# The first layer of the compression by three products per pair of units, and five K steps per turn

## What is computed

```python
def compress(rows, pos_emb, w1, w2):          # rows: B, L, groups (2), 64
    n_units = L // CMP_STRIDE                 # units of 16 tokens
    n_cmp = n_units - CMP_UNITS + 1           # a block is two adjacent units
    units = rows[:, :n_units * CMP_STRIDE].reshape(B, n_units, CMP_STRIDE, G, D)
    blocks = jnp.concatenate([units[:, j:j + n_cmp] for j in range(CMP_UNITS)], axis=2)
    hid = jax.nn.silu(jnp.einsum('bnlgd,lde->bnge', blocks + pos_emb[:, None, :], w1))
    return jnp.einsum('bnge,ef->bngf', hid, w2)
```

## Time and profile before

| | |
|---|---|
| time, median of 3 runs | 790.75 us (786.97 to 792.52) |
| span of the profiled execution | 792.1 us |
| TensorE busy | 735.8 us, 93% of the span |
| VectorE, ScalarE, GpSimd busy | 55%, 26%, 10% |
| DMA | 220.72 MB, mean 279 GB/s |

### The profile page before, as it was taken

How to read it: one execution, slowest core, us unless ns; L and a number is a source line. 1 busy time by engine, 2 the same in 40 slices (tenths; PEclk the granted TensorE clock), 3 DMA queues, 4 the chain that set the end, 5 groups by cost and what they waited for, 6 DMA issues and landing times.

```text
span 792.1 us, 14734 instructions
## 1 busy us (share of the span) xinstructions
PE 735.8 (93%) x4779; PEld 356.7 (45%) x4779; DVE 438.4 (55%) x945; ACT 206.8 (26%) x524; POOL 82.9 (10%) x155
## 2 busy tenths in 40 slices
PE   7999999999999999998999996898897887999997
PEld 3465645453545456443544562334443452433542
DVE  3351250805704357997563838957768656645273
ACT  0411011102010213122233323534455334333200
POOL 0000000000000000020002016500746200000000
PEclk9999999999999999998999997999999976999999
DMA  8997987999898989979788129988899939984621
GB/s 327 306 319 214 339 279 253 298 353 351 296 371 282 378 314 365 373 262 390 254 282 279 37 92 305 334 304 275 250 317 318 296 131 387 364 280 142 262 112 55
DMA packets 134552, 220.72 MB, mean 279 GB/s; under 512 B 17642, under 2 KB 58771, under 8 KB 133259
## 3 DMA queue, kind: packets, MB, share of 16 engines
q1 hardware_dynamic: 113754, 194.75, 71.7%
q0 software_dynamic: 6080, 13.25, 5.0%
q10 hardware_dynamic: 14640, 11.77, 4.8%
HBM read 213.84 MB, written 10.04 MB: 283 GB/s over the span
## 4 chain that ended last, share of the span: by engine, by line
PE 57%; DVE 17%; SPq 10%; DMA 8%; issue 4%; ACT 2%; POOL 0%; ACTq 0%; DVEq 0%
PE banks L652 13%; PE banks L630 13%; SPq L428 8%; PE banks L905 4%; PE banks L1036 4%; PE banks L666 4%; DMA proj<-in_cmp_cache 3%; PE banks L1157 3%; DVE att L1863 3%; DMA ring<-in_dv_cache 3%; PE banks L934 2%; PE banks L976 2%; PE banks L952 2%; DVE banks L1862 1%; PE banks L969 1%
## 5 line engine op out<-in xcount | busy, mean ns | idle before, releaser
L652 PE MATMUL banks<-ring,xt 128*128 128x512 f32 (+1 forms) x448 | 188.4, 574 | 0.0
L652 PEld LDWEIGHTS banks<-ring,xt 128*128 128x128 f32 x448 | 83.8, 192 | 93.8 <-issue 91.1
L630 PE MATMUL banks<-proj,wide 128*64 128x256 f32 x896 | 99.9, 384 | 2.2 <-DMA proj<-in_cmp_cache 2.1
L1382 ACT ACTIVATE wide<-banks,att 128x384 f32<-128x384 f32 (+3 forms) x128 | 66.4, 524 | 133.4 <-DVE att L1863 132.2
L630 PEld LDWEIGHTS banks<-proj,wide 128*64 128x64 f32 x896 | 66.3, 139 | 38.2 <-DMA proj<-in_cmp_cache 5.8
L905 PE MATMUL banks<-ring,small 128*32 128x512 f32 x512 | 71.6, 640 | 4.9 <-DMA ring<-in_dv_cache 3.3
L1589 DVE TENSOR_SCALAR small<-small 128x510 f32<-128x510 f32 x8 | 3.4, 427 | 122.8 <-ACT small L1227 106.3
L1212 ACT ACTIVATE proj<-banks,x_rs 128x512 f32<-128x512 f32 (+1 forms) x32 | 21.2, 664 | 177.0 <-PE banks L652 142.1
L666 PE MATMUL banks<-ring,small 128*32 128x512 f32 x512 | 61.4, 598 | 2.1 <-DMA ring<-in_dk_cache 2.0
L934 PE MATMUL banks<-proj 64*128 64x384 f32 (+7 forms) x256 | 54.7, 505 | 6.9 <-ACT wide L1382 6.9
L446 POOL DMA_DIRECT2D ring<-in_sel_cache x104 | 55.4, 533 | 32.9 <-issue 28.9
(11 more groups left out here) (360 smaller groups left out, 829.9 us busy)
## 6 DMA issues: line engine op xcount, KB each, us to landing
ring<-in_dk_cache SPq DMA_DIRECT2D x256, 256.0 KB, 5.7
ring<-in_dv_cache SPq DMA_DIRECT2D x256, 256.0 KB, 5.5
proj<-in_cmp_cache SPq DMA_DIRECT2D x144, 128.0 KB, 3.9
ring<-in_w_in SPq DMA_DIRECT2D x6, 2048.0 KB, 12.1
proj<-in_cmp_cache ACTq DMA_DIRECT2D x80, 128.0 KB, 5.4
ring<-in_x_nat SPq DMA_DIRECT2D x2, 2048.0 KB
ring<-in_cmp_cache SPq DMA_DIRECT2D x32, 128.0 KB, 4.2
ring<-in_w_out SPq DMA_DIRECT2D x2, 2048.0 KB, 11.9
```

The costliest lines, as they stand in the source:

```text
L630: last = mm(to, w1[:, kv, half, lp, :], rows[:, kv, g, lp, :, :, :], start=lp + half == 0, stop=lp == LP - 1 and half == 1, tile_position= ...
L652: last = mm(banks[:, 3 + n % 2, 0:width(c)], xt[:, k, P * t:P * t + P], w_ring[:, c % 2, k, 0:width(c)], start=k == 0, stop=k == KC - 1)
L1382: last = A(e_slot(j, c)[:, 0:n], banks[:, 2 * (j % 2) + c, 0:n], ACT.Exp, bias=row_max[:, j % 4, c:c + 1], accum_out=row_sum[:, j % 4, c:c ...
```

## The change

The units are paired: even unit 2m, odd unit 2m+1. Three products are taken: W1 on the even units (E), W0 on the odd ones (O), and W0 + W1 on their sum (S). Then block 2m+1 is O(m) + E(m+1), and block 2m is S(m) - O(m) - E(m). Each product has 16 matmuls of 256 columns (128 pairs x 2 groups); keys and values now go to the two column halves. The page layout in memory is changed on the host for this.

- first_layer(b) is the first two products. After two K steps first_sums(b) does the third, and only its last matmul signals pre_ready. It waits for units_summed.
- VectorE: sum_units(b) copies E out of PSUM and adds the odd units to the even ones in place (4096 columns); keep_pre(b) makes the sums and the difference in the hidden buffer; then the silu as before. W0 + W1 is made once, in the memory of the query blocks, which are cleared after sequence 7 instead of at the start.
- ScalarE's exponentials (and its half of the page loads behind them) wait for pre_kept, the last of these.
- The prompt's compression keeps both halves of w1, with 32 matmuls of 64 columns for 64 of 32.
- K_TURN is 5 instead of 6, K_LAST 5 instead of 4; the late tiles have 34 K steps over 13 tiles instead of 30 over 12. keep_scores(1), (3), (5), (6) and (7), silu_z(27) and sum_new(7) change places on VectorE, load_w(6) and load_w(7) on SyncE.

```diff
--- before.py
+++ after.py
@@ -128,9 +128,9 @@
-    w2b = z((2, 2, 64, 2, 64), w2.dtype)
-    w2b[:, 0, :, 0], w2b[:, 1, :, 1] = w2, w2
-    cmp_kv = x["cache_nsa_cmp_kv"][0].reshape(n_pool, 8, LP, 2, 2, NKV, HD)
+    w2b = z((2, 64, 2, 64), w2.dtype)
+    w2b[0, :, 0], w2b[1, :, 1] = w2[0], w2[1]
+    cmp_kv = x["cache_nsa_cmp_kv"][0].reshape(n_pool, 4, 2, LP, 2, 2, NKV, HD)
...
-        "w2": f(w2b.transpose(1, 2, 0, 3, 4).reshape(P, 2, P)),
-        "cmp_cache": f(cmp_kv.transpose(0, 3, 6, 4, 5, 2, 1).reshape(n_pool, P, 256)),
+        "w2": f(w2b.reshape(P, P)),
+        "cmp_cache": f(cmp_kv.transpose(0, 4, 7, 5, 3, 2, 1, 6).reshape(n_pool, P, 256)),
...
+        bias = sb("bias", [P, 2])
+        q_both = sb("q_both", [P, 1024])
...
+        w1_sum = q_both[:, :].rearrange("p (k l e) -> p k l e", k=2, l=LP)
+        q_nsa = q_both[:, 0:512].rearrange("p (b n) -> p b n", b=DEC)
+        q_sel = q_both[:, 512:1024].rearrange("p (q n) -> p q n", q=16)
...
-        K_STEPS, K_TURN, K_LAST = 64, 6, 4
-        K_LATE = (2, 2, 2, 2, 3, 3, 3, 2, 3, 3, 3, 2)
+        K_STEPS, K_TURN, K_LAST = 64, 5, 5
+        K_LATE = (2, 2, 2, 2, 3, 3, 3, 3, 3, 3, 3, 3, 2)
...
-                if n == 45:
+                if n == 41:
...
-                if n == 56:
+                if n == 53:
...
+            def cmp_rows_of(b):
+
+                return cmp_home[int(b == 1)].rearrange("p t (b k l q x) -> p k l q t b x", b=8, k=2, l=LP, q=2)
+
+            def first_product(b, bank, at, weights, parity):
+
+                for lp in range(LP):
+                    for kv in range(2):
+                        to = banks[64 * kv:64 * kv + 64, bank, at:at + 256].rearrange("p (t b x) -> p t b x", t=TILES, b=8)
+                        last = mm(to, weights[:, kv, lp, :], cmp_rows_of(b)[:, kv, lp, parity, :, :, :], start=lp == 0, stop=lp == LP - 1,
+                                  tile_position=(0, 64 * kv), skip_group_check=True)
+                return last
+
...
                 if b > 0:
-                    pe.wait_ge(s("hid_ready"), b)
-                rows = cmp_home[int(b == 1)].rearrange("p t (g k h l n) -> p k h l t g n", g=8, k=2, h=2, l=LP)
-                for kv in range(2):
-                    for lp in range(LP):
-                        for half in range(2):
-                            for g in range(2):
-
-                                to = banks[64 * g:64 * g + 64, kv, 1 - half:1 - half + UNITS].rearrange("p (t b n) -> p t b n", t=TILES, b=8)
-                                last = mm(to, w1[:, kv, half, lp, :], rows[:, kv, g, lp, :, :, :], start=lp + half == 0,
-                                          stop=lp == LP - 1 and half == 1, tile_position=(0, 64 * g), skip_group_check=True)
-                last.then_inc(s("pre_ready"), 1)
+                    pe.wait_ge(s("pre_kept"), b)
+                first_product(b, 0, 0, w1[:, :, 1, :, :], 0).then_inc(s("even_done"), 1)
+                first_product(b, 1, 0, w1[:, :, 0, :, :], 1).then_inc(s("odd_done"), 1)
+
+            def first_sums(b):
+
+                pe.wait_ge(s("units_summed"), b + 1)
+                first_product(b, 0, 256, w1_sum, 0).then_inc(s("pre_ready"), 1)
...
+            first_sums(0)
...
+            first_sums(1)
...
+                first_sums(b)
...
+                    for lp in range(LP):
+                        for half in range(2):
+                            for kv in range(2):
+                                to = banks[64 * kv:64 * kv + 64, 5, 256:384].rearrange("p (g n) -> p g n", g=2)[:, :, 1 - half:1 - half + P_UNITS]
+                                rows = p_rows[:, :, :, 16 * kv:16 * kv + 16].rearrange("p t u (g l) -> p l g t u", g=2)[:, lp, :, :, :]
+                                last = mm(to.rearrange("p g (t u) -> p g t u", t=TILES),
+                                          w1_again[:, 2 * kv + half, HD * lp:HD * lp + HD], rows,
+                                          start=lp + half == 0, stop=lp == LP - 1 and half == 1, tile_position=(0, 64 * kv),
+                                          skip_group_check=True)
...
 
-                act.wait_ge(s("pre_ready"), b + 1)
-                if b > 0:
-                    act.wait_ge(s("hid_ready"), b)
-                for kv in range(2):
-                    last = A(sig[:, kv, 0:NCMP], banks[:, kv, 1:1 + NCMP], ACT.Exp, bias=bias[:, 1, kv:kv + 1], scale=-1.0)
-                last.then_inc(s("exps_ready"), 1)
+                act.wait_ge(s("pre_kept"), b + 1)
+                A(sig[:, :, 0:NCMP], hid[:, :, 0:NCMP], ACT.Exp, bias=bias[:, 1:2], scale=-1.0).then_inc(s("exps_ready"), 1)
...
-            V.memset(q_nsa[:, :, :], 0.0)
-            V.memset(q_sel[:, :, :], 0.0)
...
+            V.tensor_tensor(w1_sum, w1[:, :, 0, :, :], w1[:, :, 1, :, :], ALU.add)
...
+                return V.scalar_tensor_tensor(h, pre, bias[:, 0:1], sg, ALU.add, ALU.mult)
+            both = sig.rearrange("p g n -> p (g n)")[:, 0:256]
+
+            def sum_units(b):
+
+                dve.wait_ge(s("even_done"), b + 1)
+                if b > 0:
+                    dve.wait_ge(s("hid_ready"), b)
+                V.tensor_copy(both, banks[:, 0, 0:256])
+                units = cmp_home[int(b == 1)].rearrange("p t (n q x) -> p q t n x", q=2, x=8)
+                V.tensor_tensor(units[:, 0, :, :, :], units[:, 0, :, :, :], units[:, 1, :, :, :], ALU.add).then_inc(s("units_summed"), 1)
+
+            def keep_pre(b):
+
+                to = hid.rearrange("p g (m q) -> p q g m", q=2)
+                odd, whole, even = (x.rearrange("p (m g) -> p g m", g=2) for x in (banks[:, 1, 0:256], banks[:, 0, 256:512], both))
+                dve.wait_ge(s("odd_done"), b + 1)
+                dve.wait_ge(s("units_summed"), b + 1)
+                if b > 0:
+                    dve.wait_ge(s("rows_ready"), b)
+                L(V.tensor_tensor(to[:, 1, :, 0:P - 1], odd[:, :, 0:P - 1], even[:, :, 1:P], ALU.add))
+                L(V.tensor_tensor(both, banks[:, 1, 0:256], both, ALU.add))
+                dve.wait_ge(s("pre_ready"), b + 1)
+                V.tensor_tensor(to[:, 0, :, :], whole, even, ALU.subtract).then_inc(s("pre_kept"), 1)
...
+                h = hid[:, :, 0:NCMP]
+                hidden(h, sig[:, :, 0:NCMP], h).then_inc(s("hid_ready"), 1)
...
+            def compressed(b):
+
+                sum_units(b)
+                keep_pre(b)
+                a_hidden(b)
...
-            a_hidden(0)
+            compressed(0)
...
-            a_hidden(4)
-            keep_scores(1)
+            compressed(4)
             means_of(1, early_tmp)
             norm_of(1, early_tmp)
-            a_hidden(5)
+            compressed(5)
+            keep_scores(1)
...
-            a_hidden(7)
-            keep_scores(3)
-
+            compressed(7)
+
+            L(V.memset(q_both[:, :], 0.0))
...
+            keep_scores(3)
...
-            keep_scores(5)
...
+            keep_scores(5)
...
-            keep_scores(6)
...
+            keep_scores(6)
...
+            silu_z(27)
+            sum_new(7)
...
-            silu_z(27)
-            sum_new(7)
```

More of the change, by code:

```diff
@@ L638, in second_layer @@
                     pe.wait_ge(s("rows_kept"), b)
-                for kv in range(2):
+                for g in range(2):
                     for nt in range(2):
-                        last = mm(banks[:, 2, 256 * kv + P * nt:256 * kv + P * nt + P], hid[:, kv, P * nt:P * nt + P],
-                                  w2[:, kv, :], start=True, stop=True)
+                        last = mm(banks[:, 2, 256 * g + P * nt:256 * g + P * nt + P], hid[:, g, P * nt:P * nt + P],
+                                  w2[:, :], start=True, stop=True)
                 last.then_inc(s("rows_ready"), 1)
@@ L698, in _ @@
             for kv in range(2):
-                for g in range(2):
-                    last = mm(banks[64 * g:64 * g + 64, 2, kv:kv + 1], pos_sum[:, kv, :], ones[:, 0:1],
-                              start=True, stop=True, tile_position=(0, 64 * g))
+                last = mm(banks[64 * kv:64 * kv + 64, 2, 0:1], pos_sum[:, kv, :], ones[:, 0:1],
+                          start=True, stop=True, tile_position=(0, 64 * kv))
             last.then_inc(s("bias_ready"), 1)
+            first_sums(0)
             pe.wait_ge(s("new_normed"), 1)
@@ L819, in _ @@
                     pe.wait_ge(s("new_proj_used"), 7)
-                    for kv in range(2):
-                        for lp in range(LP):
-                            for half in range(2):
-                                for g in range(2):
-                                    at = 256 + 64 * kv + 1 - half
-                                    last = mm(banks[64 * g:64 * g + 64, 5, at:at + P_UNITS].rearrange("p (t u) -> p t u", t=TILES),
-                                              w1_again[:, 2 * kv + half, HD * lp:HD * lp + HD], p_rows[:, :, :, 16 * kv + 8 * g + lp],
```

(14 more changed lines are left out.)

59 lines of the change are left out of this document (27 added, 32 removed).

## The result

The changed kernel takes 801.5 us (median of 4 runs, 800.11 to 805.84) against 791.15 (4 runs): ratio 1.0151, interval 1.0114 to 1.0188. It is slower by 1.5%, where I had forecast 794 us and no change. The profiled execution took 800.11 us, 1.7 more than its span of 798.4. That span is 6.3 above the one of before; the medians differ by 10.35. So the traces can explain 6.3 of it. The other 4 are where the two profiled executions stand among their runs. The one of after is the lowest, 1.4 under its median. For the one of before the profile gives no time; with the same 1.7 us added to its span of 792.1 it took 793.8 (an estimate), 2.65 above its median.

The account below looks back on a forecast made before the run. TensorE and the page load were taken as level, so saved TensorE work returns as waiting. Terms -0.6 - 2.55 + 0.35 + 0.3 + 5.45 = +2.95 us on the 790.75 median gave 794 us, range 786 to 801.

Parts of the forecast that it names:

- Four K steps go there: Late tiles: four more K steps at 0.925 us each, one hidden in a TensorE wait, the three others costing 2.8 us.
- Late total +5.45: Late tiles: K steps, later score copies and the prompt's compression together add 5.45 us.
- Start: Up to first layer of sequence 2: third product waits for VectorE's sum, yet sequence 2 starts 0.6 us earlier.
- Five turns: Turns from sequence 2 to 7: 179.6 us against 182.15, -2.55, with R to F kept at 110.35.
- The 1.7 for VectorE at sequence 5: Third product at b=5 waits for VectorE's sum behind norms of key heads: 1.7 us, between 0 and 3.2.
- Sequence 7 and queries: Last first layer, 12.35 + 2.0 against 14.0, +0.35; placement of queries waits longer on VectorE, +0.3.
- The prompt's compression: Late tiles: half as many matmuls, twice as wide, of 3.95 us, saving 1.9 us.
- 1: Turns: load follows traffic, one K step less shortens R to F by 2.8 us; 773 us, chance 0.13.
- 2: Turns: load has slack and TensorE sets the turn, all waits and clock losses go; 769 us, chance 0.07.
- 3: Start and sequences 3 to 7: six waits cost 3.1 us of slow clock each; 804 us, chance 0.22.
- 4: First layers: no TensorE work saved, a product costs 2 x 3.5 us; above 840 us, chance 0.02.
- the 1.6 us that I worked out by it for the short ones: Turns: if short waits also pay 1.7 us of slow clock, the total would be 1.6 us higher.

Follow-up runs that it names:

- (2): The kernel before (four products, old turns) with its last two late K steps at tile 28 instead of tiles 26 and 27: 797.37 us, ratio 1.0093.
- (1): The changed kernel with its last K steps at tiles 26 and 27 (4 each), none at tile 28: 795.26 us, 1.0066 against the kernel before.
- (3): The changed kernel with the selected blocks issued ahead of V loads 2 and 3, no K step moved: 798.71 us, 1.0098 against the kernel before.
- experiment 6: The changed kernel with unused matmuls ahead of TensorE's wait for pages, to keep the clock: 801.29 us, 1.0162 against the kernel before.
- experiments 9: The changed kernel with K steps ended by tile 27 and all 16 SyncE pages ahead of the turn's K loads: 789.66 us, 0.9991 against the kernel before.
- experiment 10: Changed kernel, K steps ended by tile 27, pages first, VectorE's compressed(5) ahead of norm_of(1): 781.04 us, 0.9862 against the kernel before.
- 4: Three products with all of the old schedule (six K steps per turn, 30 late over 12 tiles): 787.29 us, 0.9937 against the kernel before.

## Why the prediction was wrong

**The step that failed** is "Four K steps go there", and that the sum ends with "Late total +5.45": all that comes behind tile 31 stands in it at nothing, and no reason is given. I costed these steps on TensorE, and their copies on VectorE. That left out what else moves with them: a K step also releases its ring slot, and behind that release stand V loads 0 to 3, 56 block loads of 0.9 us and V load 4 in SyncE's one queue. The runs show it from both sides: the move alone costs the kernel before 0.9% (2), taking it back gives the changed kernel 6 us (1), and freeing the queue without moving a K step takes 7.1 us out of the stretch (3), though only 2.8 off the median. In the profiled executions the stretch costs 8.7 us, 4.8 as waiting for the V load and 4.0 as slow clock behind it, where all that comes ahead of it stands at +0.3.

**The single terms.**
- *Start*: -0.6 forecast, -0.4 measured (86.31 for 86.72). TensorE's wait for VectorE was 7.05 us, not 5.6, and the third product there took 5.14 at low clock.
- *Five turns*: -2.55 forecast, -4.6 measured. From R to F the load stood (110.35 forecast, 108.7 measured), F to R was 12.6 without the clock for 12.35, the waits were 15.7 for 16.7, the clock cost 5.8 at sequences 3 to 6, as forecast, and 1.3 for 2.0 at sequence 7: 3.79, 4.22 and 4.39 us of waiting cost 3.0, 2.8 and 1.3, and 2.04 and 1.23 us cost nothing. The 1.7 for VectorE at sequence 5 did not show: the slow clock covered it (the sum is ready at 204.35, the third product starts at 204.41). In the kernel of experiment 6, where the clock is kept, it shows with 3.0. Those two terms could not both be paid, and I added them.
- *Sequence 7 and queries*: +0.65 forecast, +0.4 measured (to the end of the second layer), which is luck. "12.35 + 2.0 against 14.0" sets a first layer with two K steps against one with none, and leaves out that the turn has five K steps instead of four. With all of them it is 12.35 + 2.8 + 2.0 against 14.0 + 3.7, or -0.55. In its place there was a wait of 1.14 us for VectorE ahead of line 615, and the clock cost 1.3 instead of 2.0.
- *Late tiles*, up to the end of tile 31: +5.45 forecast, +5.0 measured (from -4.7 to +0.3), but by other parts. The prompt's compression brought 0.1 us instead of 1.9, a mistake of arithmetic: half as many matmuls of twice the width are the same number of columns. The copy keep_scores(4) moved as forecast: it runs 2.0 us behind the end of tile 20 (322.87), before 2.5 ahead of it (323.11), with VectorE idle for 3.8 ahead of it. Of the 3.7 forecast for it, 2.4 appear, as TensorE's waits for what stands behind the copy: 1.24 for the sum of new rows and, at line 805, 1.16 for the softmax. The store of p_cmp lengthened nothing: the wait for the rows fell from 1.61 to 0.67, so one K step was hidden there, as forecast. The wait for the last score copy was 0.81 (0.85 forecast).

```profile
326.60 0.71 PE L799 MATMUL banks<-k_new,small 128*32 128x1 f32 x64 [1.24 <-DVE sample L1575]
...
378.93 3.82 PE L841 MATMUL banks<-proj 128*64 128x64 f32 x64
...
430.35 3.92 PE L880 MATMUL banks<-picked,proj 64*128 64x32 f32 x64 [0.81 <-DVE wide L1643]
```

**The rivals.** 1 and 2 (R to F becomes shorter, 773 and 769) fall: R to F is the same with five K steps as with six. 3 (the clock, 804) had the right side and nearly the number, for a wrong reason: its six waits, priced at 3.1 each, cost 8.5 in all, no more than the 9.8 of my own sum, and experiment 6 kept the clock in the turns and gained nothing. The slow clock that does bear on the result stands behind the V load, where the rival did not look. 4 (no TensorE work saved) falls with 7.13 us for two products. The rule of the Trainium skill that I weighed ("TensorE: Matmul & The Clock Gate", "HAM oscillation — how this bites in real kernels") is borne out in part: the trace has the slow clock behind the three longest waits of the turns and not behind 2.04 and 1.23 us, where the granted clock stayed at full speed. The waits that the Trainium skill describes there are as long as the three long ones here, so the 1.6 us that I worked out by it for the short ones went beyond what it says. What the slow clock cost in the turns was nothing that experiment 6 could recover.

**What was right**: that the K step taken out stood behind the last page in the queue, so that TensorE's saved work in the turns would come back as waiting. I left it at that; the same reading says what to do, and experiments 9 and 10 did it: pages first, then the K loads.

**What stays open**: why experiment 3 brings 2.8 us of the 7.1 that it takes out of the stretch; its 12 runs lie at 796.1 to 803.2, so the profiled execution (799.85) is no outlier. And the rest of the new schedule: without K steps at tile 28 the changed kernel (1, 795.26) is still 8 us above three products in the old schedule (4, 787.29). In the profiled executions it is 1.4 ahead at the end of tile 31, loses 2.5 in the stretch, where the slow clock lasts longer, and 4.9 behind it; no run parts the places of the score copies and weight loads from the number of late K steps. That the queue delays V load 4 and that TensorE pays for it behind tile 31 is shown by experiments 1 to 3. That all 4.0 us of slow clock come from the wait is argued: in experiment 1, with no wait at the fifth V step, the same work (from 485.61 to 498.09) still took 2.6 us longer than before, on the slow clock.

## What to carry to other kernels

When a step moves, follow the slot that it frees as well as its work: list what waits for that release in each queue and what is queued behind it, down to the first transfer that the next stage needs. Work taken off an engine that runs level with a load is worth what the load's order lets through: here the same three products brought 0.6% in one order of the loads and, against four products in the same schedule, 2.4% in another (0.9862 / 1.0108). And don't add the slow clock to a wait of another engine that runs beside it: at sequence 5 only the later of the two was paid.

## What the runs showed of the hardware

- 128 matmul records with 32 columns took 3.95 us, 64 records with 64 columns 3.82 us: between these two sizes the time goes by the columns, 31 and 60 ns a record.
- An in-place addition of 4096 columns took 4.42 us on VectorE, nearly twice the 2.29 of 2048 columns, also with the DMA share at 1.09 (47.4 to 51.9).
- Waits of TensorE for a load of 3.79, 4.22 and 4.39 us were followed by a granted clock of 0.50, 0.50 and 0.57 (1.2 GHz for all or most of the window read), one of 2.04 us by the full clock (2.4 GHz). The length of the wait alone does not sort them: in experiment 10 a wait of 2.23 us was followed by a third product of 5.36 us, in experiment 6 one of 3.01 by 3.67, the time at full clock. Windows of after, columns as in rows 3:

```profile
120.60:124.00 3.40, 3.40 (x16) 1.91 (x18) 0.00 (x0) 0.00 (x0) 0.00 (x0) 0.50 1.06 388
157.90:161.50 3.60, 3.60 (x34) 2.44 (x36) 1.97 (x3) 0.00 (x0) 0.00 (x0) 1.00 1.05 386
```

- SyncE's loads of selected blocks, 52 of them, took 44.5 to 47.7 us in every kernel, 0.9 us each, whereas the compressed pages went out at 0.56 (16 in 9.03 us, experiment 10).
- Behind the same wait of 5.67 us for ScalarE the granted clock was 0.50 in all three kernels read. It was back soon after 488.2 in the kernel before (0.96 over 488.2 to 498.1), between 490.0 and 493.4 in experiment 1 (0.63), and, with the wait of 5.08 us between, between 503.0 and 507.2 in the changed kernel (0.70).
